# Attention core of a decoder layer with five of the next head pair's nine projections run inside it as slices

## What is computed

```
x = x + 0.5 * SwiGLU(RMSNorm(x))                      # FFN 1, width 2816
P = RMSNorm(x) @ w_in    # q/k/v of 3 dilation groups | RWKV-7 rows | 2 gates
A = dilated sliding-window attention, groups (window, step) (128,1), (512,4), (2048,16):
    q = rmsnorm(q), k = rmsnorm(k) per head (8 heads of 64)
    s = q.k/8 - slope * distance, softmax over all three groups together, o = p @ v
R = RWKV-7 time mixing
x = x + w_out( sigmoid(gA) * (A @ w_a) + sigmoid(gR) * (R @ w_r) )
x = x + 0.5 * SwiGLU(RMSNorm(x))                      # FFN 2
```

## Time and profile before

| | |
|---|---|
| median of 3 runs | 2079.09 us (2074.35 to 2079.69) |
| profiled execution | 2082.03 us, its span 2080.2 us |
| mean granted TensorE clock | 0.921 |
| busy: PE, DVE, ACT, POOL | 1871.9, 757.5, 626.5, 530.6 us |
| attention, first projection to last output copy | 1017.0 to 1525.7 us |

### The profile page before, as it was taken

How to read it: one execution, slowest core, us unless ns; L and a number is a source line. 1 busy time by engine, 2 the same in 40 slices (tenths; PEclk the granted TensorE clock), 3 DMA queues, 4 the chain that set the end, 5 groups by cost and what they waited for, 6 DMA issues and landing times.

```text
span 2080.2 us, 42446 instructions
## 1 busy us (share of the span) xinstructions
PE 1871.9 (90%) x17032; PEld 1751.7 (84%) x17032; DVE 757.5 (36%) x1120; ACT 626.5 (30%) x828; POOL 530.6 (26%) x206
## 2 busy tenths in 40 slices
PE   7999999977898989878687978889789999999998
PEld 6999999977797978765585958769588999999998
DVE  3331133234625353523543342433445733203320
ACT  4331122224232413110242332314334433213321
POOL 2334344322121202000030211203113334434442
PEclk9999999988999999975797977969789999999999
DMA  4333333313121212110153451524534333323342
GB/s 145 124 125 119 114 121 121 126 64 120 50 94 46 84 44 99 38 65 21 55 195 134 164 202 56 208 104 164 201 127 162 101 122 121 138 100 121 123 137 113
DMA packets 50503, 237.49 MB, mean 114 GB/s; under 512 B 6864, under 2 KB 7504, under 8 KB 48848
## 3 DMA queue, kind: packets, MB, share of 16 engines
q1 hardware_dynamic: 44176, 219.40, 30.3%
q10 hardware_dynamic: 6208, 16.37, 2.0%
HBM read 217.98 MB, written 71.76 MB: 139 GB/s over the span
## 4 chain that ended last, share of the span: by engine, by line
issue 83%; POOL 12%; PE 3%; POOLq 1%; ACT 0%; ACTq 0%
POOL w_lo L318 12%; PE ps L331 3%; POOLq L630 0%; POOLq L317 0%; POOLq L1988 0%; POOLq L633 0%; ACT w_hi L313 0%; POOLq L318 0%; POOLq L629 0%; ACTq L312 0%; POOLq L2138 0%
## 5 line engine op out<-in xcount | busy, mean ns | idle before, releaser
L318 POOL TENSOR_TENSOR w_lo<-w_raw,w_hi 128x1024 fp32r<-128x1024 f32 (+1 forms) x202 | 530.4, 2626 | 1527.9 <-ACT w_hi L313 1527.9
L331 PE MATMUL ps<-h_hi,w_hi 128*128 128x288 f32 x2464 | 548.3, 304 | 39.2 <-DVE h_lo L453 11.2
L331 PE MATMUL ps<-h_lo,w_hi 128*128 128x288 f32 x2464 | 531.5, 297 | 0.0
L331 PE MATMUL ps<-h_hi,w_lo 128*128 128x288 f32 x2464 | 531.4, 298 | 0.0
L331 PEld LDWEIGHTS ps<-h_hi,w_hi 128*128 128x128 f32 x2464 | 401.2, 191 | 54.3 <-issue 23.1
L331 PEld LDWEIGHTS ps<-h_hi,w_lo 128*128 128x128 f32 x2464 | 400.9, 191 | 0.0
L331 PEld LDWEIGHTS ps<-h_lo,w_hi 128*128 128x128 f32 x2464 | 400.8, 190 | 0.0
L313 ACT ACTIVATE w_hi<-w_raw 128x1024 fp32r<-128x1024 f32 (+1 forms) x204 | 226.3, 1109 | 434.5 <-PE ps L331 415.5
L331 PE MATMUL ps<-g_hi,w_hi 128*128 128x288 f32 x704 | 151.6, 297 | 0.1
L331 PE MATMUL ps<-g_hi,w_lo 128*128 128x288 f32 x704 | 151.1, 296 | 0.0
L331 PE MATMUL ps<-g_lo,w_hi 128*128 128x288 f32 x704 | 151.0, 296 | 0.0
(11 more groups left out here) (360 smaller groups left out, 2104.8 us busy)
## 6 DMA issues: line engine op xcount, KB each, us to landing
w_raw<-in_w SPq DMA_DIRECT2D x172, 512.0 KB, 3.5
w_raw<-in_w SPq DMA_DIRECT2D x32, 704.0 KB, 4.0
kv<-in_kc SPq DMA_DIRECT2D x32, 576.0 KB, 6.8
kv<-in_vc SPq DMA_DIRECT2D x32, 576.0 KB, 8.1
cache_out<-in_cache SPq DMA_DIRECT2D x28, 576.0 KB
kvT<-qkv ACTq DMA_DIRECT2D x4, 1728.0 KB, 9.3
gates<-gate_out ACTq DMA_DIRECT2D x16, 288.0 KB, 2.1
gate_in<-gates SPq DMA_DIRECT2D x8, 576.0 KB, 5.1
```

What stands on the lines that cost most here:

```text
L318: nc.gpsimd.tensor_tensor(w_lo[par_][:, 0:words], w_raw[par_][:, 0:words], w_hi[par_][:, 0:words].bitcast(F32), ALU.subtract).then_inc(lo_ ...
L331: last = nc.tensor.matmul(ps[:, b + c, 0:HC], w[par_][:, wk], a[:, k, c * HC:(c + 1) * HC], start=(first and k == 0), stop=(end and k == n ...
```

## The change

Five of a head pair's nine units (`AHEAD = 5`) are now computed inside the core of the pair before it, a few slices at a time (`fill`), and the other four ahead of its own core (`own_slices`), with the norms in between. The first pair's five are computed ahead of everything; the last pair's core has no slices. The core is brought down to six banks (one pair of score banks instead of two, turns in 6 and 7, the sample's scores in 7, 2 and 3), and banks 0 and 1 take the slices (`FBANK`). Squares are now taken from the copied q or k in SBUF, into two buffers, with two root buffers and the norm's banks 4, 5 and 6, 7. The loops over head pairs are written out. The unit order changes so that both far value units come early. The store of `kvT` is three DMAs. The 20 cache copies of attention are issued in the RWKV stage, two behind each of five weight pairs in each of two rounds. The long sample scores come ahead of `scores(0)`, the short ones behind it.

```diff
-QKV_ORDER = ((0, 0), (0, 1), (1, 2), (2, 2), (1, 0), (1, 1), (2, 0), (2, 1), (0, 2))
+QKV_ORDER = ((0, 0), (1, 2), (2, 2), (1, 0), (2, 0), (0, 1), (1, 1), (2, 1), (0, 2))
+AHEAD = 5
+NORMS = (0, 3, 5, 4, 6, 7)
-        SBANK = ((4, 5), (6, 7))
-        TBANK, OBANK = (0, 1), (2, 3)
+        SBANK, TBANK, OBANK, FBANK = (4, 5), (6, 7), (2, 3), 0
+        SAMPLE_BANK = (7, 2, 3)
+        OWN_BANK = (2, 0, 2, 0)
+        NORM_BANK = (4, 4, 6, 4, 6, 4)
...
+            for hp in range(CT):
+                def fill(slices, of=hp + 1):
+                    if of == CT:
+                        return
+                    for _ in range(slices):
+                        n, k = filled // KD, filled % KD
+                        P, q = at_unit(of, n)
+                        b = FBANK if of else 2 * (n % 2)
+                        if k == 0:
+                            unit_wait(pe, P, q)
+                            if of:
+                                Pb, qb = at_unit(of, n - 1)
+                                pe.wait_ge(evac[qb], Pb + 1)
+                        last = unit_slice(q, h_hi, h_lo, k, k, KD, b)
...
+                if hp == 0:
+                    fill(AHEAD * KD, 0)
+                own_slices(0, 0, 2)
+                norm(0)
+                own_slices(0, 2, 6)
+                turn_residues()
+                own_slices(0, 6, 8)
+                for n, i in ((1, 1), (2, 3)):
+                    own_slices(n, 0, 2)
+                    norm(i)
+                    own_slices(n, 2, 4)
+                    norm(i + 1)
+                    own_slices(n, 4, 8)
+                own_slices(3, 0, 3)
+                norm(5)
+                own_slices(3, 3, 8)
+                turn_values()
...
+                    sample_long()
                     scores(0)
-                    sample_scores()
+                    sample_short()
                     scores(1)
-                    for n in range(4): turn(n); scores(n + 2) if n + 2 < 4; mix(n)
+                    fill(6); turn(0); scores(2); fill(2); mix(0)
+                    turn(1); scores(3); fill(6); mix(1)
+                    turn(2); fill(2); mix(2)
+                    turn(3); fill(6); mix(3)
...
+                    sample_turn(0); sample_turn(1); fill(2); sample_turn(2)
                     # transposes of the block results
+                    fill(6)
                     # half 0 of the sample outputs
+                            fill(2)
                     # half 1
+                    fill(3)
                     # transposes of the sample outputs
+                    fill(5)
```

(Short statements are put on one line here, and comments stand for unchanged code.) ACT's and DVE's orders, and SP's, written out in the same way:

```diff
+                if hp == 0: take(0, n) for n in range(5)      # copy out, then split the weights of the unit after next
+                square_of(0); square_of(1); store of values 1, 2; guess(0); take(hp, 5); square_of(2); guess(1)
+                square_of(3); guess(2); take(hp, 6); square_of(4); guess(3); guess(4); take(hp, 7)
+                square_of(5); guess(5); take(hp, 8); store of value 0; store of keys
+                exps(0); sample exponential; exps(1); turned(0); ahead(0); exps(2); turned(1); exps(3); turned(2)
+                ahead(1); turned(3); sample_turned(0); sample_turned(1); ahead(2); sample_turned(2); ahead(3); ahead(4)
...
+                v_place(1); v_place(2); apply(0); permuted(); v_out(2); apply(1); apply(2); apply(3)
+                spread(); apply(4); apply(5); v_out(0)
+                sample_bias(1); sample_bias(2); biased(0); sample_bias(0); maximum; biased(1); turned(0)
+                biased(2); scaled(0); turned(1); biased(3); sample scaling; scaled(1); turned(2); scaled(2)
+                turned(3); scaled(3)
...
                     copy_cache(sp, 2, 49 + 7 * cc + i)
+                    if i < 5:
+                        copy_cache(sp, 1, 8 + 10 * cc + 2 * i)
+                        copy_cache(sp, 1, 9 + 10 * cc + 2 * i)
...
+                at_load(9 * hp + 7)
+                keys_in(0, 3)
+                at_load(9 * hp + 8)
+                keys_in(3, 6)
+                at_load(9 * hp + 9)
+                keys_in(6, 8)
+                for a in range(10, 13):
+                    at_load(9 * hp + a)
+                values_in(0, 4)
+                at_load(9 * hp + 13)
+                values_in(4, 8)
+                at_load(9 * hp + 14)
+                at_load(9 * hp + 15)
```

More of the change, by code:

```diff
@@ L260, in build @@
             work = sb(c, "work", [128, 4, NT])
-            asq, ary, art = (work[:, i] for i in (0, 1, 3))
+            asq, art = (work[:, 0], work[:, 2]), work[:, 3]
             SB = work[:, :, :].rearrange("p a n -> p (a n)")[:, 0:NKEY]
@@ L1593, in mix, with sample_turn @@
                         last.then_inc(sem("block_mixed"), 1)
+                    sample_long()
                     scores(0)
-                    sample_scores()
+                    sample_short()
                     scores(1)
-                    for n in range(4):
-                        turn(n)
-                        if n + 2 < 4:
-                            scores(n + 2)
-                        mix(n)
-                    pe.wait_ge(sem("sp_ready"), hp + 1)
-                    for tl in range(3):
+                    fill(6)
+                    turn(0)
+                    scores(2)
+                    fill(2)
+                    mix(0)
+                    turn(1)
+                    scores(3)
+                    fill(6)
+                    mix(1)
+                    turn(2)
+                    fill(2)
+                    mix(2)
+                    turn(3)
+                    fill(6)
+                    mix(3)
+                    def sample_turn(tl):
                         if tl == 2:
@@ L1706, in att_dve @@
+            act.wait_ge(sem("far_v_stored"), 16 * CT)
+            act.wait_ge(sem("kv_stored"), 32 * CT)
         def att_dve(dve):
@@ L1714, in att_dve, with apply @@
             dve.wait_ge(sem("mask_loaded"), 16)
-            with dve.Fori(0, 2) as cc:
-                for c2 in range(2):
-                    hp = 2 * cc + c2
-                    def apply(n):
-                        g, kind = QKV_ORDER[n]
-                        rsqrt_dve(own, dve, RS_ATT + 6 * hp + q_index(n) + 1, bank2(4), ary, art, 3)
+            for hp in range(CT):
+                if True:
+                    def apply(i):
+                        g, kind = QKV_ORDER[NORMS[i]]
+                        rsqrt_dve(own, dve, RS_ATT + 6 * hp + i + 1, bank2(NORM_BANK[i]), ary[i % 2], art, 3)
                         a = QKV[:, g, kind, :]
-                        V.scalar_tensor_tensor(a, a, P1("qg" if kind == 0 else "kg", g), ary, ALU.mult, ALU.mult)\
+                        V.scalar_tensor_tensor(a, a, P1("qg" if kind == 0 else "kg", g), ary[i % 2], ALU.mult, ALU.mult)\
                             .then_inc(sem("qk_applied"), 1)
@@ L1763, in att_dve @@
                     dve.drain()
-                    for n in range(9):
-                        g, kind = QKV_ORDER[n]
-                        if kind < 2:
-                            apply(n)
-                        elif g:
-                            v_place(n)
-                        if kind == 2 and g != 1:
-                            v_out(g)
-                        if (g, kind) == (0, 0):
-                            permuted()
-                        if (g, kind) == (2, 0):
-                            spread()
+                    v_place(1)
+                    v_place(2)
+                    apply(0)
+                    permuted()
+                    v_out(2)
+                    apply(1)
+                    apply(2)
+                    apply(3)
+                    spread()
+                    apply(4)
+                    apply(5)
                     def biased(n):
```

396 lines of the change are left out of this document (239 added, 157 removed).

## The result

The changed kernel takes 1981.87 us (median of 4 runs, 1976.63 to 1984.75) against 2078.68 us (2074.35 to 2079.69) for the kernel before on the same chip: ratio 0.9535, 95% interval [0.9509, 0.9561]. It is 97 us faster. The forecast was 2011 with a range of 1993 to 2040, so the direction was right and the size too small; the time lies 11 us under the range.

What follows compares the result with a forecast made beforehand. Projections were taken as bound by TensorE's work, cores by a chain between engines at part clock. Attention 508.7 to 427, gain 82 less 13 allowance, +1 RWKV: -68 from 2082.03, so 2014 profiled, 2011 median; range 1993 to 2040.

Steps and rivals of the forecast that it cites:

- the RWKV row: RWKV stage of the kernel before: slices between small matmul bursts, PE busy 7.3 of 10 us, clock 1.00; model for filled cores.
- rival (a): Three filled cores: clock stays at the low level, +119 against -68, so 2130 us; chance 5%.
- The rule of the Trainium skill: Filled cores: frequent short idles between matmul groups, as bank groups take turns, can make the clock oscillate; no size given.
- Rival (c): Filled cores: slices wait for the single bank pair, four handovers a core at 2 us, +24, 2035 us; chance 14%.
- Rival (b): Ahead of each core: ACT and DVE bound, norms one after another, 47 us instead of 38, +36, 2047 us; chance 14%.
- the part on the clock: Filled cores: slices hold the full clock as in RWKV; mixes and transposes alone do not raise it (0.50 from 1248 to 1260).
- The allowance of 13 us: Attention: small waits at 2.5 us a pair, plus 1 us of low clock for each filled core.
- PE's own work in the core: Core matmuls without slices, at full clock: taken as 31 us, between 26.6 and 42.2; 0.7 more for score banks.
- The walk of the bare core: Last pair's core without slices: 50 us against 57.6 now, first wait gone, shared score banks give some back; bounds 44 and 58.
- the walk ahead of the cores: Four units left before each core: 35.1 us of PE plus waits of 1.4, 0.5 and 1.0, so 38.0 us.
- The moved copies: RWKV stage: 20 cache copies behind weight loads, slack 7.9 us against 3.5 to land, cost 1 us, bounds 0 and 10.
- Rival (d): Moved copies delay RWKV's weights by 10 us and keys or values come late in attention: +15, 2026 us; chance 7%.

Runs made afterwards that it cites:

- experiment 7: Changed kernel with each norm on PE made to wait until DVE has read the root of the norm before it: 1998.7 us, ratio 0.9623.
- experiment 4: Changed kernel with the next pair's five units as one block behind each core, no slices in it, two bank pairs for the units: 2007.45 us, ratio 0.967.
- experiment 2: Kernel before with only the 20 cache copies moved from attention to the RWKV stage: 2085.64 us, ratio 1.0046.
- Experiments 9: Kernel before with one DVE reordering in the core, bias 2 ahead of scaling 0 and bias 3 ahead of scaling 1: 2048.58 us, ratio 0.9841.
- 10: Kernel of experiment 4 with DVE's old order: bias 2 behind scaling 0, bias 3 and copy 1 later too: 2036.39 us, ratio 0.9786.
- 6: Kernel of experiment 4 with the wait for the last norm ahead of each core restored by the old order there: 2033.78 us, ratio 0.9798.
- Experiments 5: Kernel before with 26 unused matmuls of 128 columns in PE's 6.55 us wait ahead of each core: 2065.17 us, ratio 0.995.
- experiment 3: Changed kernel with the 20 cache copies issued behind the last load of RWKV's sample stage: 1970.98 us, ratio 0.9493.
- experiment 1: Changed kernel with the 20 cache copies put back into attention, five a head pair behind weight loads: 1973.76 us, ratio 0.9512.

## Why the prediction was wrong

**What it had right.** The filled cores run at the full clock without a wait of PE, as the RWKV row had said; rival (a), the clock staying low, did not come. The rule of the Trainium skill that the prediction weighed (page TensorE: Matmul & The Clock Gate, section "A second HAM failure mode: psum-queue depth-cycling") did not bite in them: the granted clock is 1.00 in all three. Rival (c), slices waiting for the single bank pair, has no row. Rival (b) has none either, and experiment 7 shows the mechanism that would have brought it. The 3.44 us of issue at the jump back are gone with the loop. One premise of the part on the clock does not hold, though the choice made with it was right: that the level does not rise by mixes and transposes alone. In the third core of experiment 4, with no projection in it, four matmuls of a mix take 1.12 us at 1332.93 and the eight transposes right behind it 1.09 at 1334.22, which is their time at the full level; PE had been without a wait since 1325.84.

**Which steps failed.** The mechanism in the filled core was right; what failed are sizes in the sum, nearly all to one side. The allowance of 13 us for small waits and low clock had nothing to pay. PE's own work in the core, with the wait for the score banks, was put at 31.7 us and measured 28.7 (9 us over three cores). The walk of the bare core gave 50 us and 41.4 was measured (8.6), and the walk ahead of the cores gave 38.0 where 35.8 to 35.9 was measured (8.6 over four). One step failed in its mechanism and to the other side: the moved copies, taken as 1 us by the slack of the weight loads, cost 10.9 by a transfer that the prediction did not look at, ACT's gate stores.

**The sum, term by term** (forecast against the windows after):

| term | forecast | measured | difference |
|---|---|---|---|
| first pair: five units, ahead, filled core | 34.0 + 38.0 + 63.7 | 34.3 + 35.8 + 60.7 | -4.9 |
| second and third pair, each | 38.0 + 63.7 | 35.9 + 60.7 | -5.1, twice |
| fourth pair: ahead, bare core | 38.0 + 50 | 35.8 + 41.4 | -10.8 |
| allowance for small waits and clock | 13 | 0 | -13 |
| RWKV and its parts | +1 | +10.9 | +9.9 |

Together -29.0: the 2014 forecast for a profiled execution becomes 1985, and 1983.89 was measured. The gain of attention was forecast as 69 us and is 107.5; that the whole is off by 29 and not by 39 is luck, since the 9.9 us lost in RWKV go the other way. The lower end of the forecast's own range doesn't come out of its terms either: 16 us for the core's work and 6.5 for half the allowance, both off 2011, make 1988.5, not 1992. The time lies under that as well. Step by step:

- **The core's own work**, taken as 31 us, is 28.7 (60.7 less 40 slices of 0.80), and there is no wait of 0.7 for the score banks in a filled core. That is the full difference of 3.0 for each of them. The bound "everything proportional to the clock", 26.6, was nearer than it was taken for.
- **Ahead of the core**, 38.0 was forecast and 35.8 to 35.9 measured. The walked waits were 1.4, 0.5 and 1.0; the rows have 1.10, 0.30 and 0.74. The own work was 33.7, not 35.1, mostly since the 9.5 us beside the units had been taken from a stretch that holds 1.2 us of waits (67.2 less 66.03).
- **The allowance** of 13 us for small waits and low clock had nothing to pay: the walk's steps were all that was there.
- **The moved copies**, taken as 1 us with a bound of 10, cost 10.9. The prediction set the median landing of weights, 3.5 us, against a slack of 7.9. That slack held: even the loads that took 10.6 and 10.5 us had landed before their split. What it had left out is that ACT waits for its own gate stores at the end of each part of RWKV. With three copies just issued two of these stores took 7.0 and 8.2 us instead of 2.3 and 3.3, and ACT waited for them (experiment 2). Rival (d) had RWKV's weights delayed by 10 us: its size came true, by another path. Its other part, keys or values late in attention, did not come. The Trainium skill, page DMA: Bandwidth & Descriptors, section "Queues, rings and completion order", says that on each DMA engine the descriptors of one ring are consumed in ring order. The trace agrees as far as it goes: the slowest two loads of the execution are ones that stand behind three copies on SP's queue. But the stores that cost the time stand on ACT's queue, with no copy ahead of them there, so the order within a queue does not tell of them.
- **The bare core**, with 8.6 us the largest error of any single stretch, has its cause in the diff. The prediction names what changes in it, the first wait gone and the shared score banks, and comes from 57.6 to 50. DVE's new order, bias 3 ahead of scaling 1, is in the diff, and neither the walk nor the rivals give it a price. Experiments 9 and 10 price it at 24 to 33 us of the whole, 6 to 8 us a core.

**Where the 97 us come from**, by the experiments: some 70 are there with no slice in the core (experiment 4), and 26 to 28 come when the slices move in. Of the 70, the early bias is worth 24 to 33 (9 and 10), and the wait ahead of the core, gone by putting norm 5 earlier and the long sample scores first, 26 (6). The jump back is 3.4. RWKV's 11 go the other way, so some 19 to 28 more are left to the rest of the new order (a wait for the sample maximum of 0.79 instead of 2.26 among it); they were not taken apart, and the parts were measured on different kernels, so this sum is rough.

Experiments 5 and 9 bear on one more point, what holds the clock of today's core down. With the 6.55 us wait ahead of it filled, the third core behind that wait runs at 0.75 instead of 0.66; with the wait kept and the one at the third mix nearly gone, it runs at 0.79. Each has a part, and the waits inside the core gave more of the time (30.4 us against 9.6).

## What to carry to other kernels

Before work is moved in to cover an engine's waits, ask of each wait what its releaser stood behind: here two steps of DVE in the wrong order held up ACT and PE, and putting them right in the old kernel gave 30 us, as much as 120 slices did in the new one (26 to 28). When a wait on TensorE lies between bursts of small matmuls, price it with the work after it as well as with its length. Before large copies are moved into a stage, list every transfer that an engine waits for in it, stores and other queues too, and read the slowest landing of each rather than the median; here the loads had room and a store of 288 KB had not. In the sample stage, behind the load of the states, the same copies cost nothing that could be told (experiment 3).

## What was not expected of the hardware

- The same kind of wait costs very differently by its place. The 23.3 us of waits at the start of four cores cost 26.3 in all (experiment 6). The 11.7 us of waits for `pt` that experiment 9 took away were worth 30.4, and with them the granted clock in the third core rose from 0.68 to 0.79. What sets the clock apart in the two cases isn't shown.
- One and the same bare core, in the same order, ran at 0.79 (41.4 us, after), 0.87 (39.5, experiment 3) and 0.95 (36.7, experiment 1). The runs don't show what decides between them.
- Twenty copies of 576 KB cost 10.9 us in RWKV and nothing measurable in attention, where the DMA engines are busier (shares of 0.34 to 0.50 with the copies in it, against 0.19 from 470 to 1005 us before). With the copies in attention (experiment 1) the loads of cached keys take 9.7 us in the median instead of 5.9, and PE has no new wait of over 0.3 us; in RWKV one kind of store took 8 us instead of 3, and its issuer was waiting. How busy the engines are did not tell where a copy hurts; which transfer was waited for did.
